# Expert stage and layer stage in one block, and the experts' down matrices issued on ACT's queue

## The reference, cut to what matters

```python
# first model, its end
hn  = rms_norm(h, norm_moe_w)
ffn = hierarchical_moe(hn, ...)            # router, then per block of tokens of expert e:
#     hid = silu(xb @ w1[e]) * (xb @ w3[e])   w1, w3: 1024 x 512
#     y   = hid @ w2[e]                       w2:     512 x 1024
h = h + ffn                                # each token: its two experts' y, weighted
h = rms_norm(h, norm_final_w)
# second model, its start
h = layer_norm(h, ln0_g, ln0_b)
for l in range(2):
    proj = h @ w_in[l]                     # 1024 x 1736
    ...                                    # three mixers, w_out, layer_norm, gated FFN, layer_norm
```

## Time and profile before

| what | us |
|---|---|
| time, median of 3 runs (3172.26 to 3173.99) | 3172.7 |
| time of the profiled execution | 3175.93 |
| its span, first to last instruction | 3174.1 |
| PE busy in the span | 2838.7 (89%) |
| PE waiting for an expert's load at L1306, 31 times | 243.4 |
| first up matmul of the experts, from the span's start | 889.64 |
| first projection matmul of the layers | 1837.76 |

### The profile page before, as it was taken

One profiled execution on the slowest core, in us unless ns is written; L12 is line 12 of the kernel. 1 busy time (PEld: TensorE's weight loads), 2 busy tenths in 40 slices (PEclk: granted clock), 3 DMA queues, 4 the chain that ended last, 5 costly groups with the idle time before them and its releaser, 6 DMA issues. The chain is left out here.

```text
span 3174.1 us, 32637 instructions
## 1 busy us (share of the span) xinstructions
PE 2838.7 (89%) x13358; PEld 1767.4 (56%) x13358; DVE 1071.1 (34%) x2331; ACT 487.1 (15%) x1116; POOL 663.3 (21%) x547
## 2 busy tenths in 40 slices
PE   8999999999976766776776799999999999999998
PEld 7888766544842322332332365558884565488853
DVE  2222222101242222222222232465554334365554
ACT  1222332210100000000000032221110214111100
POOL 1111023301100000000000030055546400275554
PEclk9999999999988888888888899999999999999999
DMA  4121121121499999999999742223330222233210
GB/s 167 60 74 67 61 87 53 60 87 55 152 380 428 427 428 427 427 428 428 427 426 428 310 149 73 67 80 113 111 114 9 89 82 81 72 113 103 97 60 27
DMA packets 136406, 581.39 MB, mean 183 GB/s; under 512 B 16314, under 2 KB 87482, under 8 KB 108226
## 3 DMA queue, kind: packets, MB, share of 16 engines
q1 hardware_dynamic: 136258, 579.30, 46.4%
HBM read 569.75 MB, written 4.28 MB: 181 GB/s over the span
## 5 line engine op out<-in xcount | busy, mean ns | idle before, releaser
L1306 PE MATMUL bank<-arena 128*32 128x512 f32 x2048 | 288.3, 724 | 243.4 <-DMA arena<-in_moe_w 243.4
L2811 PE MATMUL bank<-arena 128*128 128x256 f32 x2240 | 484.9, 378 | 0.1
L2811 PEld LDWEIGHTS bank<-arena 128*128 128x128 f32 x2240 | 424.0, 189 | 61.7 <-issue 1.4
L429 PE MATMUL bank<-arena 128*128 128x384 f32 x1280 | 432.5, 490 | 1.0 <-PEq L856 1.0
L429 PEld LDWEIGHTS bank<-arena 128*128 128x128 f32 x1280 | 298.2, 238 | 106.2 <-issue 6.7
L1306 PEld LDWEIGHTS bank<-arena 128*32 128x32 f32 x2048 | 79.6, 130 | 451.1 <-issue 445.6
L2945 POOL TENSOR_TENSOR arena<-arena 128x512 f32<-128x512 f32 x200 | 259.1, 1309 | 194.8 <-PE bank L2811 194.5
L2839 PE MATMUL bank<-arena 128*128 128x512 f32 x616 | 265.7, 592 | 2.2 <-DMA arena<-in_w_down 2.2
L2128 PE MATMUL bank<-arena 128*128 128x512 f32 (+3 forms) x736 | 258.0, 506 | 7.8 <-ACT arena L2411 4.1
L3113 POOL MEMSET arena<- 128x1 f32 x1 | 0.1, 99 | 955.9 <-POOLq L1648 955.9
L2839 PEld LDWEIGHTS bank<-arena 128*128 128x128 f32 x616 | 116.2, 189 | 149.1 <-issue 147.8
(11 more groups left out here) (333 smaller groups left out, 3094.6 us busy)
## 6 DMA issues: line engine op xcount, KB each, us to landing
arena<-in_moe_w SPq DMA_DIRECT2D x188, 2048.0 KB, 23.3
arena<-in_w_up SPq DMA_DIRECT2D x44, 1024.0 KB, 7.7
arena<-in_w_in SPq DMA_DIRECT2D x22, 1536.0 KB, 6.8
arena<-in_w_down SPq DMA_DIRECT2D x6, 2048.0 KB, 7.7
arena<-in_w_in SPq DMA_DIRECT2D x8, 1024.0 KB, 5.7
arena<-in_moe_w SPq DMA_DIRECT2D x8, 1024.0 KB, 14.1
arena<-in_w_in SPq DMA_DIRECT2D x4, 2048.0 KB, 9.2
arena<-in_w_out SPq DMA_DIRECT2D x4, 2048.0 KB, 7.8
```

The source lines that it names most:

```text
L429: ins = pe.matmul(banks[s % 2][:, 0:CW], rows, w[:, k, :], start=(k == 0), stop=(k == KT - 1))
L1306: ins = pe.matmul(banks[pr][q:q + CAP, :], m.xt[:, k, c:c + CAP], up_view(m, slots[2 * e2 + up])[:, k, :], start=(k == 0), stop=(k == KT - 1))
L2811: ins = pe.matmul(out, weights[:, k, :], rows[:, k, :], start=(k == 0), stop=(k == KT // 2 - 1))
```

## The change

Three things are done. First, `moe_block` and `layers_block` become one block, `experts_and_layers`: each engine goes from its expert function to its layer function without the meeting of all engines. Second, SP no longer issues the two down matrices of the pairs 1 to 31; ACT issues them, on its own queue, right after the SiLU of the pair before. Third, at the seam, the norm's rows and the layers' first weights are issued by SP before the experts are done; the last scatter's banks are given another order; the adds of the last group move into the layer part and stand tile by tile among the norm's steps; and the two norms (the first model's last and the second's first) are taken in one step from the weighted rows, so that the first root on POOL and the scaling on DVE go. The two order pieces below take one expert pair each, with `up_done` and `down_done` as in the code.

The diff, cut to its core:

```diff
-def sp_moe(sp, m, G, A, eb_dram):
+def sp_moe(sp, m, after, G, A, eb_dram):
     def loads(i, n):
         for x in range(n):
+            if (x + WSLOT) % 6 >= 4:
+                continue
             pp, j = x // 6, x % 6
             sp.wait_ge(G["up_done" if j < 4 else "down_done"], 4 * i + pp + 1)
             load_expert(sp, m, G, A, x + WSLOT, i)
...
-    for j in range(4):
-        sp.wait_ge(G["down_done" if j < 2 else "up_done"], 4 * (NIT - 1) + (2 if j < 2 else 3))
-        half_up(sp, m, G, A, first + j, j, 0, f"e_in{first + j}")
-    for j in range(4):
-        half_up(sp, m, G, A, first + j, j, 1, "e_last")
-    for j in range(4, 6):
-        load_expert(sp, m, G, A, 18 + j, NIT - 1)
...
+    for pr in range(2):
+        sp.wait_ge(G["up_done" if pr else "down_done"], 4 * (NIT - 1) + 2 + pr)
+        for half in range(2):
+            for j in (2 * pr, 2 * pr + 1):
+                half_up(sp, m, G, A, first + j, j, half, "e_last" if half else f"e_in{first + j}")
+    sp.dma_start(after.fw, A["norm_final_w"].partition_broadcast(P)).then_inc(G["n_col"], 16)
+    sp.dma_start(after.lncol, A["ln_cols"]).then_inc(G["n_col"], 16)
+    sp.wait_ge(G["down_done"], 4 * (NIT - 1) + 3)
+    first_of_layer(sp, after, G, A, 0, 0)
+    sp.wait_ge(G["up_done"], 4 * NIT)
+    first_of_layer(sp, after, G, A, 0, 1)
+    first_of_layer(sp, after, G, A, 0, 2)
...
-SCATTER_BANKS = ((5, 6), (7, 1), (0, 2), (3, 4))
+SCATTER_BANKS = ((5, 6), (7, 1))
+LAST_BANKS = ((0, 1), (4, 5), (6, 7), (2, 3))
...
-def act_moe(act, m, G, banks):
+def act_moe(act, m, G, banks, A):
...
             act.activation(m.hs[64:128, :], banks[pr][0:64, :], ACT.Silu).then_inc(G["hs_ready"], 1)
+            if 4 * i + pp + 1 < NE // 2:
+                for j in range(4, 6):
+                    load_expert(act, m, G, A, 6 * ((pp + 1) % 4) + j, (4 * i + pp + 1) // 4)
...
 def pe_layers(pe, m, G, banks):
     ln = Need2(pe, G)
-    pe_fill(pe, m, banks[7], 40)
+    ln("added", 8 * (NGRP - 1) + 2)
+    pe_fill(pe, m, row_banks(banks, 0, 0)[0], 8)
     pe_ln_turn(pe, m, G, banks, ln, 0, 0)
...
 def act_layers(act, m, G, banks):
...
-    for t in range(T):
-        square(t)
+    square(0)
+    square(1)
     act_ln_scaled(act, m, G, ln, 0, 0)
+    square(2)
     act_ln_turned(act, m, G, banks, ln, 0, 0)
+    square(3)
     act_ln_scaled(act, m, G, ln, 0, 1)
...
 def dve_layers(dve, m, G, banks):
...
+    def weighted(t):
+        ln("n_col", 32)
+        ln("added", 8 * (NGRP - 1) + 2 * t + 2)
+        n = own(dve.tensor_tensor(m.z[:, t, :], m.h[:, t, :], m.fw, ALU.mult))
+        dve_ln_stats(dve, own, m, m.z, t, (n, n))
         ln("n_sq", t + 1)
+        own.do(dve.tensor_scalar(m.nms[:, t:t + 1], m.nss[:, t:t + 1], LN_EPS / D, LN_EPS * EPS, ALU.mult, ALU.add))
+        dve.tensor_tensor(m.nve[:, t:t + 1], m.nmv[:, t, 1:2], m.nms[:, t:t + 1], ALU.add).then_inc(G["n_var"], 1)
+
+    dve_add(dve, m, G, banks, NGRP - 1, 0, True)
+    weighted(0)
+    dve_add(dve, m, G, banks, NGRP - 1, 1, True)
     dve_ln_shift(dve, m, G, ln, 0, 0)
+    dve_add(dve, m, G, banks, NGRP - 1, 2, True)
+    dve_add(dve, m, G, banks, NGRP - 1, 3, True)
     dve_ln_turned(dve, m, G, banks, ln, 0, 0)
...
-def layers_block(nc, m, G, banks, A, out, cm_rows):
+def experts_and_layers(nc, m, after, G, banks, A, eb_dram, cleared, out, cm_rows):
     with nc.Block() as block:
...
         @block.scalar
         def _(act):
-            act_layers(act, m, G, banks)
+            act_moe(act, m, G, banks, A)
+            act_layers(act, after, G, banks)
```

More of the change, by code:

```diff
@@ L1273, in scatter @@
                     rows = slice(64 * half, 64 * half + 64)
-                    ins = pe.matmul(banks[SCATTER_BANKS[t if last else t % 2][half]][:, :], m.gt[pr][rows, tile(t)],
+                    ins = pe.matmul(scatter_bank(banks, t, half, last)[:, :], m.gt[pr][rows, tile(t)],
                                     m.yo[pr][rows, :], start=(pr == 0), stop=(pr == 1))
@@ L1343, in pe_moe @@
     gather()
-    for i in range(NIT):
-        experts(i, i == NIT - 1)
-    scatter(NGRP - 1, True)
+    for i in range(NIT - 1):
+        experts(i, False)
     pe.wait_ge(G["routed"], 1)
     n = pe.value_load(m.misc_i[0:1, 1:2], min_val=0, max_val=MORE - 1)
+    experts(NIT - 1, True)
     with pe.If(n > 0):
-        pe.wait_ge(G["added"], 8 * NGRP)
+        pe.wait_ge(G["yo_ready"], 2 * NGRP + 2)
+        pe.wait_ge(G["gt_ready"], 2 * NGRP)
         with pe.Fori(0, n) as j:
@@ L1386, in pe_moe @@
                     rows = slice(64 * half, 64 * half + CAP)
-                    pe.matmul(banks[2 * t + half][:, :], m.gt[0][rows, tile(t)], m.yo[0][rows, :],
+                    pe.matmul(banks[2 * t + half][:, :], m.ov_gt[rows, tile(t)], m.ov_yo[rows, :],
                               start=True, stop=True).then_inc(G["ov_sc"], 1)
-def act_moe(act, m, G, banks):
+            pe.wait_ge(G["ov_added"], 8 * j + 9)
+    pe.wait_ge(G["yo_ready"], 2 * NGRP + 2)
+    pe.wait_ge(G["gt_ready"], 2 * NGRP)
+    scatter(NGRP - 1, True)
+def act_moe(act, m, G, banks, A):
     turned = banks[2][:, :].rearrange("p (f c) -> p f c", f=FF // P)
@@ L1440, in pool_moe, with dve_add @@
 def pool_moe(pool, m, G, cleared):
-    pool.memset(m.hid, 0.0).then_inc(G["zeroed"], 1)
     for n in cleared:
         pool.sem_clear(G[n])
+    pool.memset(m.hid, 0.0).then_inc(G["zeroed"], 1)
+def dve_add(dve, m, G, banks, g, t, last):
+    for half in range(2):
+        dve.wait_ge(G["sc_done"], 8 * g + 2 * t + half + 1)
+        x = m.h[:, t, 512 * half:512 * half + 512]
+        dve.tensor_tensor(x, x, scatter_bank(banks, t, half, last)[:, :], ALU.add).then_inc(G["added"], 1)
 def dve_moe(dve, m, G, banks):
@@ L1570, in weighted, with add @@
         ins.then_inc(G["w_ready"], 1)
-    def add(g, last):
+    def add(g):
         if g:
@@ L1576, in add @@
         for t in range(T):
[L1577 to L1581, removed]
+            dve_add(dve, m, G, banks, g, t, False)
     def experts(i, last):
@@ L1601, in experts @@
                 if g and not pr:
-                    add(g - 1, False)
+                    add(g - 1)
                 dve.wait_ge(G["down_done"], n + 1)
@@ L1606, in dve_moe @@
     dve.wait_ge(G["zeroed"], 1)
-    for i in range(NIT):
-        experts(i, i == NIT - 1)
-    add(NGRP - 1, True)
+    for i in range(NIT - 1):
+        experts(i, False)
     dve.wait_ge(G["routed"], 1)
     n = dve.value_load(m.misc_i[0:1, 1:2], min_val=0, max_val=MORE - 1)
+    experts(NIT - 1, True)
     with dve.If(n > 0):
         dve.wait_ge(G["gather_done"], 2 * NGRP)
-        dve.wait_ge(G["added"], 8 * NGRP)
+        dve.wait_ge(G["gt_turned"], 2 * NGRP)
+        dve.wait_ge(G["added"], 8 * (NGRP - 1))
         dve.sem_inc(G["ov_step"], 1)
@@ L1699, in layer_memory @@
     m.nst, m.nmv = sp(T, 12), sp(T, 2)
-    m.nss, m.nve, m.nrs, m.nmr, m.nrms = (sp(T) for _ in range(5))
+    m.nss, m.nve, m.nrs, m.nmr, m.nms = (sp(T) for _ in range(5))
+    m.unread = Space(arena, m.raw_place)(D)
     m.nhalf2 = sp(1)
@@ L1992, in dve_ln_turned, with dve_ln_stats @@
     ins.then_inc(G["n_a1"], 1)
-def dve_ln_moments(dve, own, m, G, t, ready):
+def dve_ln_stats(dve, own, m, x, t, ready):
     for i in range(2):
@@ L2064, in sp_layer_mixer @@
     if l:
[L2065 to L2074 removed]
+        for i in range(3):
+            before(*done(6, 2 * i + 1))
+            first_of_layer(sp, m, G, A, l, i)
         before("f_down", 14)
```

133 lines of the change are left out of this document (59 added, 74 removed).

## The result

| | before | after |
|---|---|---|
| time, median of 4 runs each, us | 3173.1 (3172.3 to 3174.0) | 3258.9 (3253.6 to 3261.0) |
| profiled execution, us | 3175.9 | 3261.0 |
| its span, us | 3174.1 | 3259.2 |

The ratio is 1.027, with a 95% interval of 1.026 to 1.0284: slower by 86 us. The forecast was 3208 and the range ended at 3232, so the direction was right and the size was not.

A forecast was written before the change was run, and what follows sets the result against it. Bytes moved set the expert stage's pace. Thirty pairs at 31.0 us gave +46, the last pair -0.5, the seam -9.5: +36, so 3212 against the profiled execution and 3208 for the median; own range 3192 to 3232.

The forecast's parts named there:

- the stock: Expert stage: some 9.8 us of transfers stand ready whenever a pair's up matmuls end (U), hiding load latencies; the change spends it.
- the sharing: Expert stage: ups 3 and 4 share with the downs, complete only when all four loads are, 19.6 us after the first byte.
- the turns: Expert stage: two filled queues served by turns, read from instruction packets taking 1.2 us beside q1's 0.55; 31.0 us per pair.
- 1.0 + 19.6 + 1.3: Expert stage, from U to the next up matmuls: 1.0 us to first bytes, 19.6 for four loads, 1.3 until PE starts.
- the dearer rival: Expert stage: restart latency 3.5 us instead of 2.3, as at pair 0; 32.2 us per pair, 3245 us; chance 0.05.
- a lead of SP by ACT's SiLU: Expert stage: ACT's first DMA goes out about 0.5 us late behind its SiLU, giving 30.5 us; set against the uneven start.
- Less 2: Expert stage: 2 us off the thirty pairs because pair 1 has a full clock, up matmuls 7.09 us instead of 9.1.
- The last pair: End of expert stage: from pair 30's up matmuls to the last down matmuls, 34.9 or 33.2 us against 34.9; taken as -0.5.
- The seam: From the last scatter to the first projection matmul: 13.2 us instead of 22.9, no wait for weights; taken as -9.5.
- The order makes no difference: Rival, expert stage: SP's loads effectively go first, 29.4 us per pair stays, only the seam's -10 remains, 3163 us; chance 0.26.

The follow-up runs named there:

- The order on one queue: Kernel before, one queue, SP alone, with the two downs issued ahead of ups 3 and 4 at the end of a pair's up matmuls: 3265.6 us, ratio 1.0298.
- the exchange of roles: Changed kernel with ups 3 and 4 issued on ACT's queue and the downs on SP's: 3252.4 us, ratio 1.0246.
- the split alone: Kernel before with only ACT issuing a pair's two downs on its own queue; two blocks and the old seam stay: 3260.6 us, ratio 1.0286.
- the version with SP's old order: Changed kernel with SP issuing all loads again in the order of before; one block, early weights and new seam stay: 3166.8 us, ratio 0.9983.
- the downs late: Changed kernel with ACT issuing the downs behind its copy of the turned hidden values, some 8 us after U: 3193.9 us, ratio 1.007.

## Why the prediction was wrong in size

- **What bounds the kernel, the stock, the sharing:** right. The trace shows a share under 1 (0.93), a dry stretch before U (share 0.08 from 1023), and downs landing with the ups (21.5 and 21.9 us). The order on one queue (32.54 us per pair) shows that nothing else is needed, and the exchange of roles (32.39) that the two queues share. But the row from which I took the turns doesn't show them: a packet of q8 beside a full q1 took 1.2 us, which I read as a wait for its turn, and packets on two full queues take 0.57 and 0.61 us. Turns were my reading; what the traces show is that the two queues move about the same, 271 and 240 packets. The choice came out right, but not for this reason: that was luck.
- **The failed step is the restart, "1.0 + 19.6 + 1.3".** Measured: 23.34 us from U to the next start instead of 21.9, 1.44 more, 43 of the 51 us by which the thirty pairs were under-estimated. Of the 1.44, some 0.8 is the slow first two microseconds of a burst that the windows show; in the pair shown that is nearly all (0.9 + 0.8 + 19.6 + 1.3 = 22.6 against 22.75), and on the mean some 0.6 are left. I had this number: pair 0 in the earlier trace rows paid 3.5 us beyond its transfers for the same restart, and the mean pair pays 3.7 here (23.34 less 19.6). I called that the dearer rival, gave it 0.05 and 3245 us, and set its unevenness off against a lead of SP by ACT's SiLU. Against that rival I held that two queues should start more evenly than one. They don't: the first two microseconds move 254 GB/s at pair 0 of the kernel before, 262 with one queue and the downs first, and 254 on two queues:

```profile
897.75:899.75 2.00, 0.00 (x0) 0.00 (x0) 1.93 (x4) 0.00 (x0) 0.00 (x0) 1.00 0.89 254
1027.00:1029.00 2.00, 2.00 (x12) 0.77 (x9) 1.71 (x3) 0.00 (x0) 0.00 (x0) 1.00 1.00 262
993.00:995.00 2.00, 2.00 (x20) 2.00 (x20) 0.87 (x1) 0.00 (x0) 0.00 (x0) 1.00 0.89 254
```

- **The 0.6 that is left goes with packets on the instruction queue,** which the earlier trace rows had (36 packets on q8) and the sum put at nothing. In 13 of the 30 pairs of the changed kernel one packet of q8 starts between 1 us after U and the next up matmuls. These pairs wait 23.67 us in the mean; of the other 17 the median is 22.75, about the sum above, with three late ones (23.85, 24.91 and 26.31) that I can't explain. With the split alone the two groups don't meet: ten pairs of 23.18 to 24.20 us, twenty of 22.32 to 22.97. In the runs with the downs first and with the roles exchanged their means lie 0.7 and 0.9 us apart, with some overlap. That is found in the traces, not tested.
- **The lead for SP doesn't exist.** ACT's issue is out 0.07 us after U, 0.14 before SP's. What it would have been worth was right in kind: 1.69 us of lead gave 1.81 us per pair.
- **"Less 2" for a full clock at pair 1:** wrong. Its up matmuls took 9.80 us, not 7.09 (granted clock 0.72, not 1.00), after a wait of 10.28 us where there had been 0.83. With the up matmuls at 9.3 for 9.1 on the mean, this is the other 8 us.
- **The last pair:** -0.5 forecast, -0.6 measured, but not by the terms forecast. The second half of its up matmuls starts 24.1 us after U instead of 21.9, and it and the down matmuls take 3.65 and 3.64 us instead of 5.34 each. That they nearly cancel is luck.
- **The seam:** 13.2 us from scatter to projection forecast, 13.64 measured. The jump on PE that now stands ahead of the scatter was not in the sum and costs 2.7 (3.48 less 0.80); the first projection block took 5.40 us instead of 8.10 (granted clock 1.00 in it, 0.66 before) and gives 2.7 back. The total, -9.25 for -9.5, was right by luck: the sum left out two terms that cancel.
- **"The order makes no difference"** (0.26) needed ups 3 and 4 to land within 20.3 us of U. That point of decision holds: with one down on the second queue the next start is 20.4 us after U and the stage is back at 29.6 us per pair, with two it isn't (23.34 and 32.65). The split gained no bandwidth (432 GB/s while both queues are filled, 427 with one); it changed the order in which loads become complete, and that cost 97 us.

## What to carry to other kernels

Here, where transfers set the pace, a second queue for loads that are wanted later took its share from those that are wanted next (32.65 us per pair for 29.41). In such a place list for each wait which loads must be complete by then, and how long the rest can take before the engines run dry. Cost a queue that runs dry by a burst from idle that the trace already has, from the event to the start of the waiting engine (3.5 us beyond the transfers at pair 0 here, 3.7 in the changed kernel), and don't set that number off against a lead that no row shows. Look at what now stands between two steps in each engine's program when blocks are merged, jumps included (a gap of 3.48 us here for one of 0.80).

## Not expected of the hardware

- A burst from idle moved 0.51 MB instead of 0.85 in its first two microseconds of windows with bytes, on two queues; on one queue it was 0.51 (pair 0 before) and 0.52 (the downs first).
- With the jump over a long branch on PE ahead of the scatter, the scatter started 3.48 us after the down matmuls in the changed kernel and 2.30 us in the version with SP's old order, 0.90 there with the scatter ahead of the jump. In five traces with the jump it starts 2.76 to 2.77 us after one 16 KB packet on the instruction queue.
- Pairs with one such packet within the burst waited about 1 us longer (23.63 against 22.65 us in the mean with the split alone).
- With the downs late, short and long pairs by turns (20.1 and 42.5 us in the two shown), from loads that are all of one size.
